# Values late, loads early: a fused decoder kernel with its router, attention, norms and scan reordered

## The reference, cut to what matters

```python
h = rms_norm(x, norm_mix);  x = x + hybrid_mixer(h)      # short conv, sparse attention (NSA), gated delta rule
h = rms_norm(x, norm_ffn)                                # stage moe1
grp = argmax(h @ w_rg + b_rg);  le = (h @ w_re + b_re)[grp]      # 4 groups of 8 experts
top_p, top_i = top_k(softmax(le), 2)
gate = top_p / sum(top_p) * softmax(h @ w_rg + b_rg)[grp]
x = x + sum(gate_e * (silu(h @ w_eg[e]) * (h @ w_eu[e])) @ w_ed[e] for the 2 chosen of 32 experts)
for i in (0, 1):                                         # second block, two layers
    h = modulate(rmsnorm(x, norm_g[i, 0]), sh1, sc1)
    y = mla_mixer(h) if i == 0 else mamba2_mixer(h)      # latent attention (mla); scan (ssm)
    x = x + g1 * y
    h = modulate(rmsnorm(x, norm_g[i, 1]), sh2, sc2)
    x = x + g2 * (swiglu(h) if i == 0 else moe_swiglu(h))    # ffn; moe2, 8 experts of 2816
return rmsnorm(x, final_norm)
```

## Time and profile before

| | |
|---|---|
| three runs | 2620.5, 2620.92 and 2622.52 us, median 2620.92 us |
| the profiled execution's own time | 2633.1 us |
| its span | 2631.3 us, 29041 instructions |
| mean granted clock of TensorE | 0.894 |
| busy: TensorE, its weight loads | 2230.7 us (85%), 1662.9 us (63%) |
| busy: VectorE, ScalarE, GpSimd | 1436.3 us (55%), 1155.0 us (44%), 40.9 us (2%) |
| read from HBM | 653.60 MB, 249 GB/s over the span |

### The profile page before, as it was taken

The page is one execution under the profiler, slowest core; times in us unless marked ns, Lnnn a source line. Parts: engine busy times, 40 slices in busy tenths (PEclk is TensorE's granted clock), DMA queues, the critical chain, the costliest instruction groups (busy, mean ns, idle before and its releaser), DMA issues.

```text
span 2631.3 us, 29041 instructions
## 1 busy us (share of the span) xinstructions
PE 2230.7 (85%) x11922; PEld 1662.9 (63%) x11922; DVE 1436.3 (55%) x1992; ACT 1155.0 (44%) x1489; POOL 40.9 (2%) x107
## 2 busy tenths in 40 slices
PE   6888898766677665787799889888999999999997
PEld 6767566552222211455799777667887888878875
DVE  4744435333011000332455576557989988988997
ACT  3432333320000000242344356645777777777775
POOL 0000100000000000000000000000000000000000
PEclk9889898767777788897899889788999999999999
DMA  7451830219999999657344432134989989989994
GB/s 255 167 185 49 281 135 33 96 64 387 409 409 409 409 409 409 248 198 287 112 156 182 160 128 97 64 128 158 343 319 370 336 321 369 338 318 372 337 341 193
DMA packets 267688, 656.66 MB, mean 250 GB/s; under 512 B 13454, under 2 KB 38546, under 8 KB 267544
## 3 DMA queue, kind: packets, MB, share of 16 engines
q1 hardware_dynamic: 266592, 652.90, 67.1%
q10 hardware_dynamic: 952, 1.77, 0.2%
HBM read 653.60 MB, written 1.05 MB: 249 GB/s over the span
## 4 chain that ended last, share of the span: by engine, by line
PE 67%; DMA 16%; DVE 9%; ACT 5%; issue 2%; POOL 0%; ACTq 0%; DVEq 0%; POOLq 0%
PE psum L241 16%; PE psum L242 16%; PE psum L243 16%; PE psum L236 11%; DMA ring<-in_w_expert_up 5%; DMA ring<-in_w_expert_down 5%; DMA ring<-in_w_expert_gate 5%; PE psum L2278 2%; PE psum L1043 2%; DVE w_lo L186 2%; PE psum L835 1%; ACT w_hi L176 1%; PE psum L2300 1%; DVE xbc L841 1%; DMA ring<-in_ada_w 1%
## 5 line engine op out<-in xcount | busy, mean ns | idle before, releaser
L186 DVE TENSOR_TENSOR w_lo<-ring,w_hi 128x1024 fp32r<-128x1024 f32 (+1 forms) x778 | 904.8, 1179 | 404.0 <-ACT w_hi L176 391.0
L176 ACT CAST w_hi<-ring 128x1024 fp32r<-128x1024 f32 (+1 forms) x778 | 785.2, 1015 | 448.5 <-PE psum L243 444.9
L241 PE MATMUL psum<-w_hi,xg_hi 128*128 128x512 f32 (+1 forms) x768 | 293.9, 383 | 1.2 <-ACT xg_lo L1961 1.2
L243 PE MATMUL psum<-w_lo,xg_hi 128*128 128x512 f32 (+1 forms) x768 | 288.8, 376 | 0.0
L242 PE MATMUL psum<-w_hi,xg_lo 128*128 128x512 f32 (+1 forms) x768 | 288.7, 376 | 0.0
L2278 PE MATMUL psum<-ring,hT 128*32 128x512 f32 x1024 | 169.8, 799 | 117.3 <-DMA ring<-in_w_expert_gate 62.7
L2278 PEld LDWEIGHTS psum<-ring,hT 128*32 128x32 f32 x1024 | 32.6, 129 | 248.7 <-DMA ring<-in_w_expert_up 86.6
L241 PEld LDWEIGHTS psum<-w_hi,xg_hi 128*128 128x128 f32 x768 | 144.6, 188 | 30.5 <-issue 1.8
L242 PEld LDWEIGHTS psum<-w_hi,xg_lo 128*128 128x128 f32 x768 | 144.6, 188 | 29.0 <-issue 1.7
L243 PEld LDWEIGHTS psum<-w_lo,xg_hi 128*128 128x128 f32 x768 | 144.4, 188 | 28.5
L2130 DVE TENSOR_TENSOR x<-x,psum 128x1024 f32<-128x1024 f32 x14 | 17.1, 1221 | 244.0 <-PE psum L236 244.0
(11 more groups left out here) (653 smaller groups left out, 3838.0 us busy)
## 6 DMA issues: line engine op xcount, KB each, us to landing
ring<-in_moe_w_gate SPq DMA_DIRECT2D x40, 2048.0 KB, 9.4
ring<-in_moe_w_up SPq DMA_DIRECT2D x40, 2048.0 KB, 10.2
ring<-in_moe_w_down SPq DMA_DIRECT2D x40, 2048.0 KB, 9.2
ring<-in_w_expert_gate SPq DMA_DIRECT2D x32, 2048.0 KB, 16.7
ring<-in_w_expert_up SPq DMA_DIRECT2D x32, 2048.0 KB, 17.1
ring<-in_w_expert_down SPq DMA_DIRECT2D x32, 2048.0 KB, 17.7
ring<-in_ada_w SPq DMA_DIRECT2D x24, 2048.0 KB, 8.3
ring<-in_ssm_w_in SPq DMA_DIRECT2D x10, 2048.0 KB, 8.0
```

Source lines behind the costliest of these rows:

```text
L176: a.copy(self.buffers(n, src.shape)[0], src).then_inc(*self.hi_made.up())
L186: v.tensor_tensor(lo, src, hi.bitcast(F32), SUB).then_inc(*self.lo_made.up())
L241: p.matmul(o, l[0], r[0], start=start, stop=False)
L243: return p.matmul(o, l[0], r[1], start=False, stop=stop)
```

## The change

1. **Places beside the ring.** `Ring` gets units that are not in a slot but in a tensor of their own. Six of the twelve units of group 0 (gate 0 and 1, up 2 and 3, down 0 and 1) go to six such tensors, which share memory with `w_hi`/`w_lo`, with tensors of `nsa`, and with free room of `moe1`. SP loads two of them when `nsa` has finished and four after the last product of `proj`.
2. **Norm.** Of each four tiles ScalarE copies two (`norm_turned_act`) and VectorE two; high and low parts are made per two tiles and directly behind each four; the first consumer waits for the second half only at its fifth tile (`ready=`). The router's logits are accumulated per half (`logits_pe`).
3. **Attention.** The product with the values and the finish come one step later.
4. **moe1.** The group's softmax weight is applied beside the places product; the table is spread over groups 1 to 5.
5. **Scan.** Four convolutions first, then one low part, `cb_dve`, three low parts; `xs_act` stands directly behind the decays.
6. **by_halves_pe** awaits each part just before its use.

```diff
@@ Ring
+    def add_beside(self, src, tensor, loaded):
+        self.beside.append((src, tensor, loaded))
+        return -len(self.beside)
+
+    def load_beside(self, e, u):
+        src, tensor, loaded = self.beside[-u - 1]
+        src = src(None)
+        e.dma_start(tensor[:, :].rearrange("p (k n) -> p k n", k=src.shape[1]), src).then_inc(loaded, 16)
...
+    places = {(0, 0, 0): place_ns[0], (0, 0, 1): place_ns[1], (0, 1, 2): place_w[0], (0, 1, 3): place_w[1], (0, 2, 0): place_fe[0],
+              (0, 2, 1): place_fe[1]}
@@ norm_dve
-            for k in range(4):
+            for k in range(2):
...
-        if h is not None:
-            for k4 in (0, 4):
-                v.wait_ge(*st.act.of("h_hi", k4))
-                v.tensor_tensor(h[1][:, k4:k4 + 4, :], hT[:, k4:k4 + 4, :], h[0][:, k4:k4 + 4, :].bitcast(F32),
-                                SUB).then_inc(*st.dve.up("h", k4))
+            if h is not None:
+                for k in ((0, 2) if k4 == 0 else (2, 0)):
+                    two = slice(k4 + k, k4 + k + 2)
+                    v.wait_ge(*st.act.of("h_hi", k4 + k))
+                    v.tensor_tensor(h[1][:, two, :], hT[:, two, :], h[0][:, two, :].bitcast(F32), SUB).then_inc(*st.dve.up("h", k4))
-    def norm_split_act(a, st, h):
...
+    def norm_turned_act(a, st, h, gain, shift):
+        for k4 in (0, 4):
+            a.wait_ge(*st.pe.of("hT", k4))
+            ps = banks.of(st.name, "hT", k4)
+            for k in (2, 3):
+                a.activation(hT[:, k4 + k, :], ps[:, k * T:(k + 1) * T], ACT.Identity if shift else ACT.Copy, scale=gain(k4 + k),
+                             bias=shift(k4 + k) if shift else 0.0).then_inc(*st.act.up("hT", k4))
+            banks.empty(st.act, st.name, "hT", k4)
+            if h is not None:
+                for k in ((0, 2) if k4 == 0 else (2, 0)):
+                    a.wait_ge(*(st.act if k else st.dve).of("hT", k4))
+                    a.copy(h[0][:, k4 + k:k4 + k + 2, :], hT[:, k4 + k:k4 + k + 2, :]).then_inc(*st.act.up("h_hi", k4 + k))
@@ by_feature_pe (by_token_pe alike at k0 == 4)
+                if ready and f == 0 and k == 4:
+                    p.wait_ge(*ready)
@@ by_halves_pe
-        parts = [split.take(p, n) for n in range(split.first[u], split.end(u))]
+        parts = []
         for half, out_ in enumerate(outs):
-            for n, (hi, lo) in enumerate(parts):
+            for n in range(split.count[u]):
+                if not half:
+                    parts.append(split.take(p, split.first[u] + n))
+                hi, lo = parts[n]
@@ attention_pe (attention_dve alike: finish of m = n - AHEAD - 1)
-        for n in range(len(jobs) + AHEAD):
+        for n in range(len(jobs) + AHEAD + 1):
...
                 ins.then_inc(*st.pe.up("shown", m))
+            m -= 1
+            if m >= 0:
+                job = jobs[m]
                 p.wait_ge(*st.act.of("pT", m))
                 ps = banks.take(p, st.name, "out", m)
@@
+    def logits_pe(p, st, w):
+        ps = banks.take(p, st.name, "logits")
+        for k4 in (0, 4):
+            for signal in (st.dve, st.act):
+                p.wait_ge(*signal.of("hT", k4))
+            for t in range(NT):
+                for k in range(k4, k4 + 4):
+                    ins = p.matmul(ps[:, t * 512:t * 512 + w.shape[2]], hT[:, k, t * P:(t + 1) * P], w[:, k, :],
+                                   start=k == 0, stop=k == KD - 1)
+        ins.then_inc(*st.pe.up("logits"))
@@ groups_dve
-                table_dve(v, S["moe1"], moe1)
...
+            if 1 <= i < 6:
+                table_dve(v, S["moe1"], moe1, 3 * (i - 1), MOST_OVER_GROUPED if i == 5 else 3 * i)
@@ moe1_dve: the wait for "gs", the reciprocal and the two products move into
+        places_dve(v, st, moe1, weights_of_groups)
@@ ssm_act
+                if hh == 7 and g < 3:
+                    xs_act(a, g + 1)
                 step = ssm_step(g, hh)
...
-                    if g < 3:
-                        xs_act(a, g + 1)
@@ ssm_dve
             ssm_conv_dve(v, "x", 0, f)
-            split.make_lo(v, split.first[z0] + PARTS + f + 1)
-            if f == 1:
-                cb_dve(v)
+        split.make_lo(v, split.first[z0] + PARTS + 1)
+        cb_dve(v)
+        split.make_lo(v, split.first[z0] + PARTS + 4)
@@ ssm_pe (mix, mla and ffn wait for h 0 alike)
-        for k4 in (0, 4):
-            p.wait_ge(*st.dve.of("h", k4))
+        for signal in (st.dve, st.act):
+            p.wait_ge(*signal.of("hT", 4))
         ps = banks.take(p, "dt")
@@ sync
         start_sync(s)
+        ring.load(s, run1.units[0, 0, 2])
+        finished(s, S["nsa"])
+        for n in range(2):
+            ring.load_beside(s, run1.units[0, 0, n])
+        ring.load(s, run1.units[0, 1, 1] + 1)
+        s.wait_ge(*split.multiplied(unit["out", 1]))
+        for g, n in ((1, 2), (1, 3), (2, 0), (2, 1)):
+            ring.load_beside(s, run1.units[0, g, n])
```

More of the change, by code:

```diff
@@ L131, in loaded @@
     def loaded(self, u):
+        if u < 0:
+            return self.beside[-u - 1][2], 16
         return self.slot_loaded[u % SLOTS], 16 * (u // SLOTS + 1)
     def slot(self, u):
+        if u < 0:
+            return self.beside[-u - 1][1][:, :]
         return self.tensor[:, u % SLOTS, :]
     def empty(self, signal, u):
-        self.now[u] = signal.last()
+        if u >= 0:
+            self.now[u] = signal.last()
 class Split:
@@ L343, in block @@
     ring = Ring(ring_t, semaphore, "ring")
+    places = ExitStack()
+    place_w = [sb(f"place_w{n}", [P, UNIT], where=places) for n in range(2)]
+    places.close()
     w_hi, w_lo = sb("w_hi", [P, PARTS, PART], F32R), sb("w_lo", [P, PARTS, PART], F32R)
@@ L473, in block @@
     mT = [sb(f"mT_{n}", [P, KD, T], F32R, where=mg) for n in ("hi", "lo")]
+    sb("under_places", [P, 1248], where=mg)
+    place_ns = [sb(f"place_ns{n}", [P, UNIT], where=mg) for n in range(2)]
     mg.close()
@@ L518, in block @@
     pos_f, kq = sb("pos_f", [NT, P], where=fe), sb("kq", [P, 2, NT, 16], where=fe)
+    place_fe = [sb(f"place_fe{n}", [P, UNIT], where=fe) for n in range(2)]
     fe.close()
@@ L1474, in attention_pe @@
                 ins.then_inc(*st.pe.up("scores", n))
-            if beside:
+            if beside and n < len(jobs) + AHEAD:
                 beside(p, n)
             m = n - AHEAD
-            if m >= 0:
+            if 0 <= m < len(jobs):
                 job = jobs[m]
@@ L1530, in attention_dve @@
                 v.tensor_scalar(mx[:, n, :], mx[:, n, :], -scale, None, MUL).then_inc(*st.dve.up("max", n))
-            if beside:
+            if beside and n < len(jobs) + AHEAD:
                 beside(v, n)
-            m = n - AHEAD
+            m = n - AHEAD - 1
             if m >= 0:
@@ L2436, in moe1_pe @@
         norm_pe(p, st, xn_ffn)
-        p.wait_ge(*st.dve.of("hT", 4))
-        ps = banks.take(p, "moe1", "logits")
-        for t in range(NT):
-            ins = product(p, ps[:, t * 512:t * 512 + 36], [(hT[:, k, t * P:(t + 1) * P], w_rout[:, k, 0:36]) for k in range(KD)])
-        ins.then_inc(*st.pe.up("logits"))
+        logits_pe(p, st, w_rout[:, :, 0:36])
         places_pe(p, st, moe1)
@@ L2480, in moe1_dve, with weights_of_groups @@
         gates_dve(v, st, moe1, le)
-        v.wait_ge(*st.act.of("gs"))
-        settle(v, v.reciprocal(gs[:, :], gs[:, :]), d)
-        for t in range(NT):
-            settle(v, v.tensor_scalar(moe1.gate[:, t, :], moe1.gate[:, t, :], gs[:, t:t + 1], None, MUL), d)
-        places_dve(v, st, moe1)
+        def weights_of_groups(v):
+            v.wait_ge(*st.act.of("gs"))
+            settle(v, v.reciprocal(gs[:, :], gs[:, :]), d)
+            for t in range(NT):
+                settle(v, v.tensor_scalar(moe1.gate[:, t, :], moe1.gate[:, t, :], gs[:, t:t + 1], None, MUL), d)
+        places_dve(v, st, moe1, weights_of_groups)
         groups_dve(v)
@@ L2563, in mla_pe @@
             ps = banks.take(p, "unit", u)
-            by_token_pe(p, u, h_mla, [[ps[:, t * 512:t * 512 + w] for t in range(NT)]])
+            by_token_pe(p, u, h_mla, [[ps[:, t * 512:t * 512 + w] for t in range(NT)]], ready=None if n else st.dve.of("h", 4))
         modulation_pe(p, st, spread0)
@@ L2845, in ffn_pe @@
         norm_pe(p, st, xn_ff)
-        for k4 in (0, 4):
-            p.wait_ge(*st.dve.of("h", k4))
+        p.wait_ge(*st.dve.of("h", 0))
         for c, nf in enumerate(ff_chunks):
             for g in range(2):
-                by_feature_pe(p, unit["ff", g, c], h_ff, nf)
+                by_feature_pe(p, unit["ff", g, c], h_ff, nf, ready=None if c or g else st.dve.of("h", 4))
         pairs = [banks.take(p, "ff_down", half) for half in range(2)]
@@ L3356, in moe2_pe @@
         norm_pe(p, st, xn_moe)
-        p.wait_ge(*st.dve.of("hT", 4))
-        ps = banks.take(p, "moe2", "logits")
-        for t in range(NT):
-            ins = product(p, ps[:, t * 512:t * 512 + 8], [(hT[:, k, t * P:(t + 1) * P], w_rout[:, k, 36:44]) for k in range(KD)])
```

(2 more changed lines are left out.)

58 lines of the change are left out of this document (35 added, 23 removed).

## The result

| | before | after |
|---|---|---|
| median of the runs | 2620.81 us (2620.5 to 2622.52, 4 runs) | 2535.41 us (2531.67 to 2537.53, 4 runs) |
| the profiled execution | 2633.1 us, span 2631.3, clock 0.894 | 2536.3 us, span 2534.6, clock 0.919 |
| TensorE / VectorE / ScalarE busy | 2230.7 / 1436.3 / 1155.0 us | 2175.2 / 1426.3 / 1166.6 us |

The ratio is 0.9671, with a 95% interval of 0.9655 to 0.9688: 85.4 us faster. The forecast was 2546.9 us, with a range of 2529 to 2567.

The account below looks back on a forecast made before the run. DMA was taken to bound moe1's expert groups, TensorE or its waits the rest. Gains of 25.0, 2.4, 12, 13.5, 9.5, 7.6 and 4.0 sum to 74.0; 2620.9 - 74.0 = 2546.9 us, range 2529 to 2567.

Parts of the forecast that it names:

- Places (25.0): moe1: six units beside the ring leave 86 loads; last lands at G (group 0's first gate product) + 452.9, gain 25.0.
- The gap of 2.5: moe1, group 0: DMA pauses 2.5 us for a late fifth slot; without this pause the gain would be 27.5.
- G + 29.0: moe1: when down 2's slot comes free, counted from group 0's first gate product (G), after eight units, mid, gather, three down units.
- (a): moe1: TensorE runs group 0 at the lower clock, DMA idles 11; places give 16, total 2556 us; chance 0.10.
- (e): moe1: TensorE bounds the groups at the lower clock, 68 a group against 61.7 of transfers; total about 2636; chance 0.02.
- Sparse attention (12): nsa: taking the values product one step later removes most of 17.1 us of waits for transposed exponentials; gain 12.
- Rival (b): Both attentions: the wait moves to the pair the next scores take; they give 8 and 9, total 2555; chance 0.12.
- Latent attention (13.5): mla: six waits of 1.1 go (6.2) and the output transposes start 7.3 earlier; gain 13.5.
- rival (d): Attentions and scan: fewer waits keep the clock up beyond what was counted, by 12 us; total 2535; chance 0.10.
- Five norms (9.5, with 1.7 of the routing): Norms split over two engines: mla 3.0, ffn 3.0, scan 2.2, moe2's router 2.0, first norm -0.7; routing's copy wait 1.7.
- Rival (c): Norms: ScalarE's half brings table loads, 1.28 before and after in four; the norms' gain becomes 0, total 2556; chance 0.04.
- Scan (7.6): Scan: 3.7 from an earlier first Silu, 3.9 from xs_act passing a high part and z's copy at two group changes.

Follow-up runs that it names:

- before_again: The kernel before, unchanged, run once more for a second profile: 2620.01 us, span 2618.3.
- table0: The changed kernel with the whole table of overfull groups computed in group 0 again, as before: 2546.7 us, ratio 0.9713 to the kernel before.
- after_again: The changed kernel itself, unedited, run again as the mark for other runs: 2533.5 us, ratio 0.9664 to the kernel before.

## Why the prediction was right, and where not

The forecast was 11.5 us too high, inside the range. Undoing the three large parts one by one costs 36 + 27 + 23 = 86; all parts together brought 88 by the medians taken beside them (85.4 in the first measurement). That the total came so near is in part luck: by the table the stages of the two attentions gave 6 more each than forecast, while that of the scan gave 3.4 less and the start 1.5 less. I had also taken the 12.2 us between the profile and the median as spread over the kernel and near none of the terms. That was wrong, as 9 of them lay in the sparse attention, where they made the waits look shorter (17.7 in all, against 20.5 in before_again).

- **Places (25.0): right**, 25.3 by stage. The first slot at G + 5.4 and 5.14 us a load held, and the last load came 27.0 earlier, near the 27.5 of the case without a gap. The gap of 2.5 wasn't there: the step that failed is the sum to G + 29.0, made with a gather of 6.5, a row that stood at a clock of 0.57; it took 3.74. The last unit, 1.7 slower than before, took most of that back, so the 25.3 owe something to two errors that cancel. That the table would cost some 10 us in the new order was shown by table0 (9.5); that it cost nothing in the old one is read from the earlier trace rows and not tested. Rivals (a) and (e) are out: the transfers don't pause once the first slot is free, and no group is bound by TensorE. The gather of 13 in rival (e) was a misreading too, as the 6.5 already stood near the lower level.
- **Routing (2.4):** 1.6 between the usual execution and this one, and 3.2 against the first profile; the norm's part of it alone is 2.7 when undone. The stretch differs by 1.6 between the two profiles of before, so no more can be said, and no run tests the 0.7 of the group weight by itself.
- **Sparse attention (12): mechanism right, 18.3.** The step that was mis-sized is the sum of waits. I kept 5.1 of the waits (1.1, twice 2, and the finishes' 1 set against the clock's 1), and 5.4 are left. But the waits to begin with are 20.5 in a usual execution and not 17.1. The rest of the 18.3 after 15.1 of waits is 3.2, against the 1 that I had counted for the clock; the mean clock is 0.85 before and after, so what these 3.2 are is not shown. Rival (b) is out: there is no wait on the scores' bank.
- **Latent attention (13.5): mechanism right, about 19.5.** The eight waits of 12.3 became one of 1.3, 11.0 instead of the 13.5 of the tail and the six waits together; 8.3 less busy time in the same matmuls came with a mean clock of 0.91 instead of 0.86. I had put the clock at nothing here. This is the mechanism of rival (d), at 0.10, which had 12 from the attentions and the scan and gave 2535 for the whole. What the runs show of it is these 8.3 (12.2 in after_again) and 3.1 less busy time in the stage of the scan (0.88 instead of 0.86), together near its 12; so I had given it too small a chance. Its ground, that the products after a wait of 3 or more are the slow ones, is too simple: a unit ran at 3.28 after a wait of 1.18.
- **Five norms (9.5, with 1.7 of the routing): too small by half**, 22.6 when undone. The removed waits were sized well (mla 4.8 to 1.4, ffn 4.5 to 2.0, the router's 2.1 to 0). The products behind them ran slower before (moe2 and ffn, above), and I gave that no term. Of the 22.6 the 7.4 in mla are uncertain by some 4 us. The first norm's loss was real at its first product, 0.3 to 1.1 later than with the old norm, where I had 0.7; at the first copy the profiles of the two overlap. Rival (c) is out: 33 table loads before and 33 after, none beside the norms' Identity. A load takes 1.28, and in 22 of the 33 ScalarE goes on 0.01 behind it, so nothing further shows beside the 1.28. The Trainium skill (ScalarE: Activation LUTs, Table sets: the hidden batching unit) has identity in every set; by that, the trace agrees.
- **Scan (7.6): wrong**, 0.3 by stage beside the other parts. The step "xs_act passes one high part and the copy of z, 1.95 at two changes" failed: the decay row behind it takes the pair that z's copy empties, so the last of three operations ends when it did before. Moving z as well uncovered tmpy. The 3.7 at the first SiLU came (3.8) and was then given back, about half of it to other small waits and half to more busy time; I had taken it for granted that a lead lasts to the end of its stage. What both moves bring without the new norm and by_halves no run shows, and 5 of the stage's 10.4 us belong to no part alone.
- **by_halves (4.0):** 3.0 in its stage, and the next one was 1.0 shorter without it. The wait of 2.48 was sized right, the slow products behind it were not.

## What to carry to other kernels

Take a second profile before reading a stage's surplus: 9 us of this one's "before" belonged to one execution. When a wait of TensorE is removed, ask of the same matmuls how long they are busy in a run at the higher clock and in one at the lower; in the latent attention that came to 8.3 us beside 11.0 of waits, in the sparse attention to some 3 beside 15.1, while a single lead in a stage with many waits was given back. Windows of two kernels are to be set from the same event to the same event, and hold the same number of matmuls. Parts that lie in one stage are best also taken out two at a time, as their single costs need not add up. And before moving a copy ahead, list every bank that the consumer's next instruction takes: otherwise the wait only changes its name.

## What the runs showed of the hardware that was not expected

A stretch mostly repeats from run to run for one order of instructions (144.8 to 145.2 us in eleven profiles with the new attention order; with the old one 162.9, 163.1, and once 171.9), and yet 35 us of mla ran at a clock of 0.76 in one profile and at 0.95 in another of the same kernel. The clock doesn't simply follow the wait just ahead: 3 us less idle time ahead of the scan's norm left the next products at 0.54 (0.55 without).
